# A streaming encoder step (retention, forgetting attention, product-key experts): transposed rows, decay rows and retention outputs made another way

## The reference

```python
h = rms_norm(x, norm1_g)
rq, rk, rv, rg, fq, fk, fv, logf = project(h, w_in, ...)     # one projection, 8 heads of 64 each kind
ro, s_new = retention(rq, rk, rv, s0)                        # chunkwise, decayed state 64x64 per head
fo = softmax(fq @ fk.T / 8 + (c_q - c_k), causal) @ fv       # c = cumulative sum of logf
x = x + concat(rms_norm(ro) * silu(rg), rms_norm(fo)) @ w_out
xn = rms_norm(x, norm2_g)
q = xn @ peer_wq                                             # 8 heads x 2 halves of 128
e, g = top-16 of 128x128 key pairs per head (two top_k, then one over the sums), softmax
x = x + sum over 128 chosen experts of g * gelu(xn @ u[e]) * v[e]
```

## Time and profile before

| | us |
|---|---|
| median of three executions | 3847.42 (3836.97 to 3848.20) |
| profiled execution, its own time | 3865.37 |
| its span, first to last instruction | 3863.6 |
| TensorE busy | 2370.1 (61%) |
| VectorE busy | 2448.0 (63%) |
| ScalarE busy | 473.8 (12%) |
| GpSimd busy | 1428.5 (37%) |
| mean granted TensorE clock | 0.768 of 2.4 GHz |

### The profile page before, as it was taken

How to read it: one execution, slowest core, us unless ns; L and a number is a source line. 1 busy time by engine, 2 the same in 40 slices (tenths; PEclk the granted TensorE clock), 3 DMA queues, 4 the chain that set the end, 5 groups by cost and what they waited for, 6 DMA issues and landing times.

```text
span 3863.6 us, 34930 instructions
## 1 busy us (share of the span) xinstructions
PE 2370.1 (61%) x11957; PEld 970.8 (25%) x11957; DVE 2448.0 (63%) x6334; ACT 473.8 (12%) x1311; POOL 1428.5 (37%) x1275
## 2 busy tenths in 40 slices
PE   8999989778477566846547655684343334334333
PEld 4455445323133122314213311231010001001000
DVE  4225324989566556878966655788886555555555
ACT  2001132202022010102112200110111000000000
POOL 1001100265344443433444444434444444444443
PEclk9988999989688787967668877897666556566655
DMA  3010451899999999999999999999999999999998
GB/s 117 22 39 17 130 191 55 334 395 406 411 410 415 420 418 394 409 391 404 415 417 420 409 420 418 409 407 416 409 407 422 421 420 417 413 422 410 421 421 366
DMA packets 251073, 1357.89 MB, mean 351 GB/s; under 512 B 33792, under 2 KB 53064, under 8 KB 103440
## 3 DMA queue, kind: packets, MB, share of 16 engines
q0 software_dynamic: 165888, 1208.03, 75.8%
q1 hardware_dynamic: 84720, 147.04, 10.5%
q10 hardware_dynamic: 288, 0.59, 0.0%
HBM read 1325.22 MB, written 30.35 MB: 351 GB/s over the span
## 4 chain that ended last, share of the span: by engine, by line
DMA 36%; PE 20%; DVE 16%; POOL 8%; issue 6%; ACT 1%; another core or an unknown queue 0%; POOLq 0%; DVEq 0%; ACTq 0%
DMA M<-in_peer_uv,M 36%; PE yp L2067 12%; POOL M L1632 8%; DVE M L2352 6%; PE ab L2020 1%; PE ef L2055 1%; DVE exg L2369 1%; DVE strips L2374 1%; PE ab L1861 1%; PE c L1999 1%; PE d L1883 1%; DVE M L2119 1%; PE d L1999 1%; DVE gel L2361 1%; DVE M L2118 1%
## 5 line engine op out<-in xcount | busy, mean ns | idle before, releaser
L1632 POOL DMA_INDIRECT M<-in_peer_uv,M x1152 | 1321.8, 1147 | 1801.5 <-PE yp L2067 1445.0
L2352 DVE SCALAR_TENSOR_TENSOR M<-M 128x1024 f32<-128x1024 f32 x1152 | 1411.0, 1226 | 856.5 <-DMA M<-in_peer_uv,M 824.5
L2067 PE MATMUL yp<-M,strips 128*32 128x512 f32 x4608 | 898.5, 921 | 1279.4 <-DVE strips L2374 1253.8
L2067 PEld LDWEIGHTS yp<-M,strips 128*32 128x32 f32 x4608 | 159.2, 144 | 1888.4 <-DVE strips L2374 1490.5
L1813 ACT ACTIVATE gel<-gel 128x4 f32<-128x4 f32 x288 | 59.2, 205 | 2151.8 <-DVE gel L2363 2117.5
L2020 PE MATMUL ab<-M 128*128 128x512 f32 x576 | 264.9, 608 | 1.3 <-ACT M L1769 1.3
L426 PE MATMUL z<-M 128*128 128x512 f32 x432 | 190.1, 597 | 0.9 <-PEq L105 0.9
L2020 PEld LDWEIGHTS ab<-M 128*128 128x128 f32 x576 | 108.2, 196 | 137.6 <-issue 136.1
L1900 PE MATMUL ab<-M 128*128 128x512 f32 x288 | 130.6, 605 | 5.2 <-DVEq L2229 5.2
L867 POOL TENSOR_SCALAR small<-small 128x8 f32<-128x8 f32 x9 | 2.6, 285 | 331.7 <-DVE small L837 331.7
L426 PEld LDWEIGHTS z<-M 128*128 128x128 f32 x432 | 81.3, 191 | 97.5 <-issue 97.4
(11 more groups left out here) (248 smaller groups left out, 2517.6 us busy)
## 6 DMA issues: line engine op xcount, KB each, us to landing
M<-in_peer_wq SPq DMA_DIRECT2D x12, 2048.0 KB, 28.5
M<-in_w_in SPq DMA_DIRECT2D x9, 2048.0 KB, 11.3
M<-in_peer_uv,M POOLq DMA_INDIRECT x1152
M<-in_w_out SPq DMA_DIRECT2D x24, 512.0 KB, 23.4
M<-in_x_prompt SPq DMA_DIRECT2D x16, 512.0 KB, 10.9
x_scratch<-M SPq DMA_DIRECT2D x9, 512.0 KB
xts_scratch<-M SPq DMA_DIRECT2D x9, 512.0 KB
M<-xts_scratch SPq DMA_DIRECT2D x9, 512.0 KB
```

What stands on the lines that cost most here:

```text
L1632: nc.gpsimd.indirect_dma_start(ring[n % NR], None, a["peer_uv"], bass.IndirectOffsetOnAxis(ap=idxH[:, t % 6, s // 4, s % 4:s % 4 + 1], axis=0)
L2067: last = nc.tensor.matmul(yp[32 * j:32 * j + 32, 512 * c:512 * c + 512], strips[:, n % 2, j, :], ring[(4 * n + j) % NR][:, D + 512 * c:D + ...
L2352: nc.vector.scalar_tensor_tensor(out=row, in0=row, scalar=1.0, in1=xrep[:, s % 4, :], op0=ALU.mult, op1=ALU.mult, accum_out=dots[:, t % 2, ...
```

## The change

In retention the outputs of a tile go to one bank: eight matmuls with all 128 rows, then, one per pair of heads, a matmul of the queries of both heads with a block-diagonal copy `bd` of the state, which VectorE writes beside `st`; the scores of the two row halves are issued in turn; the gate matmuls of the sample tile come in one piece behind its outputs. In the tail the transposed rows are neither stored nor read. x1 is read once a tile into `x1b`; VectorE makes xn from it (`make_row`, before the first gather and at gather 108 of each tile), `replicate_x` multiplies slices of the identity by it, and TensorE adds x1b itself into `yp` ahead of the first `add_v` of a tile, so `finish` is a copy. The decay rows of groups 1 and 2 are spread by TensorE from a 64x128 copy of c (`spread_decay`) and copied to `cB` by ScalarE; group 0 still reads them. The loads of the front are dealt anew: keys, values and queries separately, `w_out` in part during the attention (`wload`), the first `wq` block after the transposes (`qload`). The last tile's sum is made and stored in two halves.

```diff
-            op_all = [ps(f"op{i}", [P, GW]) for i in range(2)]
-            op = [b[:, 0:PAIRS * HD].rearrange("p (r e) -> p r e", r=PAIRS) for b in op_all]
+            op = [ps(f"op{i}", [P, GW]) for i in range(2)]
+            bd = spare[:, GW:GW + PAIRS * P].rearrange("p (r e) -> p r e", r=PAIRS)
...
-                        b0 = 64 * half
-                        last = nc.tensor.matmul(sc[half][:, r, :], kT[b0:b0 + 64, r, t * P:(t + 1) * P],
-                                                qT[b0:b0 + 64, r, t * P:(t + 1) * P], start=True, stop=True)
-                    last.then_inc(sc_done, 1)
+                        for half in range(2):
+                            if s >= 1 and r == 0:
+                                pe.wait_ge(mask_done, 2 * (s - 1) + half + 1)
+                            b0 = 64 * half
+                            last = nc.tensor.matmul(sc[half][:, r, :], kT[b0:b0 + 64, r, t * P:(t + 1) * P],
+                                                    qT[b0:b0 + 64, r, t * P:(t + 1) * P], start=True, stop=True)
+                            if r == PAIRS - 1:
+                                last.then_inc(sc_done, 1)
...
+                    o = op[t % 2]
+                    if t >= 2:
+                        pe.wait_ge(oev, t - 1)
...
-                        last = nc.tensor.matmul(o, sT[:, s % 2, h % 2, r, :], vn[:, t, h * HD:(h + 1) * HD],
-                                                start=True, stop=(t == 0))
-                        if t:
-                            last = nc.tensor.matmul(o, qT[b0:b0 + 64, r, t * P:(t + 1) * P],
-                                                    st[b0:b0 + 64, r, :], start=False, stop=True)
-                        if h == NH - 1:
+                        last = nc.tensor.matmul(o[:, h * HD:(h + 1) * HD], sT[:, s % 2, h % 2, h // 2, :],
+                                                vn[:, t, h * HD:(h + 1) * HD], start=(h == 0),
+                                                stop=(t == 0 and h == NH - 1))
...
+                    if t:
+                        pe.wait_ge(st_done, t)
+                        for r in range(PAIRS):
+                            last = nc.tensor.matmul(o[:, r * P:(r + 1) * P], qT[:, r, t * P:(t + 1) * P], bd[:, r, :],
+                                                    start=False, stop=(r == PAIRS - 1))
+                        last.then_inc(o_done, 1)
...
-                        if h in (0, 1, 2, 4, 5, 6):
-                            gate(ST, h + (1 if h < 3 else 0))
...
-                for half in range(2):
-                    scores(0, half)
+                scores(0)
                 for s, t in enumerate(ORDER):
-                    for half in range(2):
-                        if s + 1 < TILES:
-                            scores(ORDER[s + 1], half)
-                        if t == ST:
-                            if half:
-                                gate(t, 0)
-                        elif s:
-                            gate(t, half)
+                    whole = s == 0 or t == ST
+                    if s + 1 < TILES:
+                        scores(ORDER[s + 1])
+                    if not whole:
+                        gate(t, 0)
+                        gate(t, 1)
...
-                    for k in range(KC - 1 if s else 0, KC):
+                    for k in range(0 if whole else KC - 1, KC):
...
-                        nc.vector.tensor_tensor(st, stt, sd, ALU.mult).then_inc(st_done, 1)
+                    new = stt if t else up
+                    for b0 in (0, 64):
+                        nc.vector.tensor_tensor(bd[b0:b0 + 64, :, b0:b0 + 64], new[b0:b0 + 64], sd[b0:b0 + 64], ALU.mult)
+                    nc.vector.tensor_tensor(st, new, sd, ALU.mult).then_inc(st_done, 1)
...
+                nc.gpsimd.memset(bd[:, :, :], 0.0).then_inc(bd_set, 1)
...
-                        for par in range(2):
-                            last = nc.scalar.copy(
-                                mixo[:, t, 0:GW].rearrange("p (r q e) -> p q r e", q=2, e=HD)[:, par], op[par])
-                        last.then_inc(oev, 1)
+                        nc.scalar.copy(mixo[:, t, 0:GW], op[t % 2][:, :]).then_inc(oev, 1)
...
+        ROW = P - 20
...
-                        add(rest, ("decay", g, h + 1), sp=(11.0 if g else 2.5, ("dve", ("foxs", g, last))))
-                wait = [("sp", ("load", g)), ("sp", ("loadq", g))] if g and n == FIRST[g] else []
+                    if h < NH - 1 and g:
+                        spread_decay(g, h + 1, ("dve", ("foxs", g, last)))
+                    elif h < NH - 1:
+                        add(rest, ("decay", g, h + 1), sp=(2.5, ("dve", ("foxs", g, last))))
+                wait = [("sp", ("load", g)), ("sp", ("loadk", g)), ("dve", ("rgate", g - 1, GT - 1))] if g and n == FIRST[g] else []
...
+                    if g:
+                        add(rest, ("wload", g, r), sp=(14.0, ("pe", ("foxs", g, n))))
...
-                    add(rest, ("loadq", g), sp=(40.0, *chosen))
+                    at = routed if nt < GT else [("sp", ("pturn", 0, 2 * LATE - 1)), ("pe", ("pmm", 0, 2 * LATE - 1, 1))]
+                    add(rest, ("loadk", g), sp=(25.0, *at))
+                add(rest, ("load", g), sp=(40.0 if g else 6.0, *routed))
+                if g:
+                    spread_decay(g, 0)
+                    spread_decay(g, 1)
...
+                        if g and i == GT - 1:
+                            add(rest, ("qload", g), sp=(42.0, ("pe", ("hturn", g, i))))
...
+                    if i % P == ROW and i // P + 1 < TILES and ("sp", ("hadd", (i // P + 1) // GT, GT - 1)) not in done:
+                        return None
...
-            xTn = M[:, 22528:23552].rearrange("p (k n) -> p k n", k=KC)
+            x1b = M[:, 22528:23552]
...
+            csd64 = causal[0:64, 0, :]
...
+                    elif kind == "loadk":
...
+                        sp.dma_start(kTg[:, :, 0:w], a["kts"][:, :, 0:w]).then_inc(kg_in, 16)
...
-                            sp.dma_start(kTg[:, :, 0:w], a["kts"][:, :, 0:w]).then_inc(kv_in, 16)
-                            sp.dma_start(vg[:, 0:w // P, :], a["new_fox_v_p"][0, 0, 0:w]
-                                         .rearrange("(t p) h d -> p t (h d)", p=P)).then_inc(kv_in, 16)
-                        load_decay(NH * g)
-                        load_decay(NH * g + 1)
-                    elif kind == "loadq":
-                        t0 = GT * g
-                        if g:
-                            sp.wait_ge(gate_done, t0)
                             sp.dma_start(fq, a["qts"][:, :, t0 * P:(t0 + GT) * P]).then_inc(fq_in, 16)
+                            load_v(range(t0 if g == 1 else 0, t0 + n))
...
+                    elif kind == "wload":
+                        sp.wait_ge(s_done, FIRST[g] + 2 * len(tiles_of(g)) * (arg[0] + 1))
+                        load_wout(g, [arg[0]])
+                    elif kind == "qload":
+                        sp.wait_ge(t_mm, GT * g + GT)
+                        load_wq(g, 0)
...
+                        if g:
+                            load_wout(g, range(4, KC))
...
-                        if g:
-                            load_wout(g)
-                        else:
+                        if g == 0:
...
-                            load_wq(g, 0)
                             load_wq(g, 1)
+                            load_wq(g, 2)
...
-                        sp.dma_start(a["xts"][t], xT[:, arg[0]].rearrange("p k n -> p (k n)")).then_inc(xT_out, 16)
...
-                def load_xTn(t):
-                    sp.wait_ge(xT_out, 16 * GT * (t // GT + 1))
-                    sp.dma_start(xTn.rearrange("p k n -> p (k n)"), a["xts"][t]).then_inc(xTn_in, 16)
+                def load_x1(t):
+                    sp.wait_ge(x1_out, 16 * GT * (t // GT + 1))
+                    if t >= 1:
+                        sp.wait_ge(x1b_used, t)
+                    sp.dma_start(x1b, a["x1"][t]).then_inc(x1b_in, 16)
...
+                sp.dma_start(csd64, a["csd"].rearrange("h (j n) -> (h j) n", j=PT)).then_inc(csd_in, 16)
...
-                    if t >= 1:
-                        sp.wait_ge(out_done, 16 * t)
-                    sp.wait_ge(x1_out, 16 * GT * (t // GT + 1))
-                    sp.dma_start(xb, a["x1"][t]).then_inc(xb_in, 16)
...
-                        sp.wait_ge(xr_ev, 8 * t + 8)
-                        load_xTn(t + 1)
-                sp.wait_ge(y_out, TILES)
-                sp.dma_start(a["y_sample"].rearrange("b t d -> (b t) d"), xb).then_inc(out_done, 16)
-                sp.wait_ge(out_done, 16 * TILES)
+                        load_x1(t + 1)
+                for c in range(2):
+                    sp.wait_ge(y_out, TILES + c)
+                    sp.dma_start(a["y_sample"].rearrange("b t d -> (b t) d")[:, 512 * c:512 * c + 512],
+                                 xb[:, 512 * c:512 * c + 512]).then_inc(out_done, 16)
+                sp.wait_ge(out_done, 16 * TILES + 16)
...
```

(69 more changed lines are left out.)

148 lines of the change are left out of this document (84 added, 64 removed).

## The result

The changed kernel takes 3814.6 us (median of 10 runs, 3810.4 to 3821.0) against 3851.7 for the kernel before on the same chip: ratio 0.9907, interval 0.9887 to 0.9928, so 37 us less. Forecast were 3773 and 74 us less, with a range up to 3812. The direction was right; half of the gain is missing, and the time lies 3 us above the range. The profiled execution took 3810.4 us (span 3808.6), 55 less than the profiled one before.

What follows compares the result with a forecast made beforehand. The tail was taken as bound by DMA bytes, mostly expert gathers, with phases in a row before it. 40 + 38 - 1.2 - 2 - 2 + 1 = 74 us less, scaled to the median: 3773 us, range 3745 to 3812.

Steps and rivals of the forecast that it cites:

- Part 3: Added work in the tail: make_row 1.2 us, borders 2, decay rows by TensorE 2; the front's new loads 0.
- The slack of 15.6 us at tile 3: Group 1's front: tile 3's last index cast ends 15.6 us before its first gather, so quicker loads gain nothing.
- C: Rival, chance 0.06: group 1's front comes late and holds tile 3's first gather; 3857 us at 100 us late.
- rival B: Tail, chance 0.20: bytes go, but later slot releases starve the gather ring; 28 us more, 3801.
- Part 1: Tail: transposed rows and decay rows no longer moved, 15.2 MB, 36 to 50 us less, taken as 40.
- Part 2: Retention: 3.4 us less a tile, 20 for six tiles, 18 for sample tile and tile 2; 38 in all.
- From one execution to the median: Whole kernel: 74 us off the profiled 3865.4 gives 3791.6; applied to the 0.5% lower median 3847.4, 3773.
- D: Rival, chance 0.12: retention gives only its low end, 17 us; 3794.
- Part 4: End of the kernel: last sum and store made in halves, 1 us less.
- the length of the stream: Sign in the tail: first to last dot product 3111 to 3118 us after the change, 3151 before.
- Wrong if: Signs of failure: tail share below 0.98, GpSimd waiting for index copies in mid-tail, or retention keeping a slow clock.

Runs made afterwards that it cites:

- e1: Kernel before with the new retention alone, its tail, planner and scratch tensors as before: 3821.5 us, ratio 0.991.
- e7: e3 with the decay rows of groups 1 and 2 read from DRAM by DMA again, as before the change: 3810.6 us, ratio 0.9891.
- e3: Changed kernel with the third query block of groups 1 and 2 loaded behind the two key blocks instead of ahead: 3790.0 us, ratio 0.9834.
- e2: Changed kernel with the front's loads (planner steps, costs, buffers, SP order) as in the kernel before: 3807.6 us, ratio 0.9881.
- e6: e3 with the third projection-weight block loaded in two halves, query stores between, and the sample's first cached keys ahead of small loads: 3778.6 us.
- e9: e6 without the eight x1 matmuls into yp ahead of each tile's first add_v, x1 left out of y: 3782.8 us, ratio 0.9821.
- e5: The kernel before itself, unchanged, run and profiled once more: 3851.0 us (3839.1 to 3880.6).
- e8: e3 with the sample tile's eight gate matmuls spread between its small matmuls again, as before the change: 3792.3 us, ratio 0.9836.

## Why the prediction was wrong, by its own steps

By the medians the change falls apart as follows: retention 29 less (e1); everything else in the tail, but with keys first and decay rows by DMA, 11 less (e1 to e7); decay rows by TensorE 21 less (e7 to e3); keys behind the query blocks 25 more (e3 to the changed kernel). Sum 36 less; measured 37.

*The step that failed* is in Part 3: the front's new loads "move bytes and remove none", "So 0, and no gain". Two terms of opposite sign stand there. The third query block was put in front of keys for which TensorE waits, and its price is 25 us (e3). And the quicker front is needed: with the old loads the front of group 1 comes late (e2), 18 us slower than e3. In sum the new loads as they were cost 7 us against the old ones (3814.6 against 3807.6), and with one line moved they gain 18.

A further 11 us (e6) have no term in the sum at all. The changed tail shifted the plan's steps, and two waits for transfers became long whose place on SP's queue had not changed: one at 851, which is there with the old loads too, and one at 1645. Part 3 priced each added operation by itself and gave all of them together some 5 us; what the shift of the plan does to waits that exist already it put at nothing, without a reason. Together with e3 this accounts for the new idle time: it was 33.6 us, and e6 has none of it.

The slack of 15.6 us at tile 3 was taken as settled, although the same sum made the stream in front of it quicker; e2 shows it 26 us quicker there. And of the loads only the bytes were counted, not what each now stands behind on SP's queue, which the diff shows line by line. The sentence that a load behind a wait can come late was written, but as a rival of one large delay at tile 3 (C, 0.06); it came as four of 5 to 16 us, each before a TensorE or ScalarE step that `add_v` or the tanh was queued behind. The effect of rival B came about (the ring starves, forecast 3801), but not by its causes: e7 clears the decay rows, e9 the x1 matmuls.

*Part 1, bytes, 40*: right. 38.3 us of engine time, 14.2 MB in the stream: 13 transfers of transposed rows fell away there, not 15, because the reads of the first two tiles came before the first gather and x1 is still read eight times behind it. The decay rows hold more than their share: 23.6 us for 7.4 MB, 3.2 a MB, and 14.7 for the other 6.8, 2.2 a MB. The decay rows came near the high bound of Part 1 (3.3) and the transposed rows below the low one (2.4), so that 40 came out right partly by luck.

*Part 2, retention, 38*: right in the matmuls, wrong in the clock. Per tile 4.4 instead of 3.4: outputs 2.9 (2.5 forecast), scores 1.1 (0.9). The 18 us for the sample tile and tile 2 rested on one execution. The two took 63.1 us there, 39.6 after the change, as forecast and more; but the kernel before took 46.3 in e5 with no change made, so that 6.7 of the 18 are the change's, all of it in tile 2 (18.9 to 12.0; the sample tile 27.4 and 27.6). Tile 2 is at the full clock after the change, but it was already at 0.86 in e5, and the order of the gates makes no difference to the sum of the two tiles (e8). So the change is worth 32 us in a like pair, 29 by the medians.

*From one execution to the median*: the change was subtracted from the profiled 3865 and the remaining 0.5% scaled away. But that surplus sat in the very stretch that the change shortens. So 18 us were counted once as a gain of retention and once as the surplus of the execution; they should have been taken out of the retention term first. Of the 37 us that are missing, the mis-sized retention term is 9 (29 for 38) and the idle time is 29 (33.6 where Part 3 had some 5); these are read from medians and from single profiles and add up no closer than a few us.

*Part 3, make_row, borders, decay rows, 5*: they don't show. e9 prices the x1 sum at none; decay rows by TensorE add no idle time (e3 29.7, e7 29.2).

*The range*: its upper end is given as B and D together. B alone is 28 us above 3773 and D alone 21, which together is 3822 and not 3812, so the stated end does not follow from the rivals' own prices.

*Part 4, the end, 1*: 10.4 us from the last dot to the end of the span before, 9.2 after: 1.2.

Of the signs given in the prediction, the length of the stream told it at once: 3146 instead of 3111 to 3118. The three named as "Wrong if" stayed silent. The share in the tail fell only from 1.01 to 1.00, not below 0.98: 33.6 us of idle time are 1% of the stream, so this bound was too coarse for a loss of nearly half the forecast gain. GpSimd did not wait for the index copies, and retention did not keep the slow clock. Queue 1 carries 16.8 MB less in all and 14.2 less in the stream, for 15.

## What to carry to other kernels

In a stream bound by bytes, price a moved load twice: what it now stands behind on its queue, at the rate that this queue gets beside the gathers (90 GB/s here, not 413), and which in-order engine waits for it with a release queued behind. When the stream gets shorter, or the plan of the work beside it is dealt anew, take that from every slack before calling a load neutral, also where the load itself has not moved: price the waits, not only the operations added. A busy share of a long stretch hides a loss of 1%; sum the idle time. A clock stretch seen in one profile is not yet a term of the sum; look at how far the plain runs spread.

## What the runs showed of the hardware

Beside 8 KB gathers a queue of 2 KB packets got as many packets as the gathers' queue (1330 against 1335 in 30 us), which is 90 of 413 GB/s. The kernel before ran 72 us of its attention at the lower TensorE clock in one profiled execution (e5) and not in the other, which cost 28 us; in the retention it was 55 us in one and 17 in the other. In all eleven kernels the stream less queue 1's engine time less idle time was 2883 to 2891 us: in this stream the engine time of the second queue came on top of the gathers' and was not hidden behind it.
